# Sparse attention with scores from three products of rounded parts, the parts made by GpSimd

## What is computed

```
q = (c_q @ w_uq).reshape(B, S, DSA_HEADS, DSA_QK_DIM)     # 16 heads of 64
...
_, idx = lax.top_k(score, topk)                            # 128 keys for each query
...
q_lat = jnp.einsum('bqhd,hdc->bqhc', q_b, w_uk)
s = jnp.einsum('bqhc,bqkc->bqhk', q_lat, kv_sel).astype(jnp.float32) * (DSA_QK_DIM ** -0.5)
s = jnp.where(valid[:, :, None, :], s, -jnp.inf)
p = jax.nn.softmax(s, axis=-1).astype(kv_sel.dtype)
o_lat = jnp.einsum('bqhk,bqkc->bqhc', p, kv_sel)
o = jnp.einsum('bqhc,hcv->bqhv', o_lat, w_uv)
...
return o @ w_out
```

## Time and profile before

| | |
|---|---|
| time, median of 3 runs | 1359.1 us (1358.92 to 1359.27) |
| profiled execution | 1357.8 us, of which the span of the trace is 1356.1 us |
| PE busy | 1294.5 us, 95% of the span |
| DVE, ACT, POOL busy | 910.8, 606.4, 160.2 us |
| mean granted TensorE clock | 0.986 of full speed |
| first scores in the trace | 865.5 us |
| steady attention, one pair of heads | 9.3 to 9.5 us |
| first matmul of the output projection | 950.7 us |

### The profile page before, as it was taken

How to read it: one execution, slowest core, us unless ns; L and a number is a source line. 1 busy time by engine, 2 the same in 40 slices (tenths; PEclk the granted TensorE clock), 3 DMA queues, 4 the chain that set the end, 5 groups by cost and what they waited for, 6 DMA issues and landing times. The chain is left out here.

```text
span 1356.1 us, 18327 instructions
## 1 busy us (share of the span) xinstructions
PE 1294.5 (95%) x6915; PEld 1062.6 (78%) x6915; DVE 910.8 (67%) x1588; ACT 606.4 (45%) x1141; POOL 160.2 (12%) x172
## 2 busy tenths in 40 slices
PE   3799999999999999999999999999999999999998
PEld 3668788889887888887788876666888888888886
DVE  4878787647566888678875759877465474457245
ACT  3256774545453332233234655587353342333231
POOL 1001120104401111102000001231010001000000
PEclk9799999989999999999999999999999999999999
DMA  9644523110508896879643120001136368336321
GB/s 323 201 166 149 193 63 94 64 62 1 187 31 323 225 241 241 242 217 242 244 166 94 39 79 32 31 32 33 62 108 174 102 145 217 111 76 155 95 92 63
DMA packets 111913, 183.56 MB, mean 135 GB/s; under 512 B 9933, under 2 KB 74714, under 8 KB 111578
## 3 DMA queue, kind: packets, MB, share of 16 engines
q1 hardware_dynamic: 87930, 107.01, 24.1%
q0 software_dynamic: 23904, 75.50, 20.1%
HBM read 178.31 MB, written 4.19 MB: 135 GB/s over the span
## 5 line engine op out<-in xcount | busy, mean ns | idle before, releaser
L411 PE MATMUL ps<-h_hi,w_hi 128*128 128x512 f32 x872 | 344.5, 395 | 0.4 <-ACT tmp L1066 0.4
L413 PE MATMUL ps<-h_hi,w_lo 128*128 128x512 f32 x872 | 341.3, 391 | 0.0
L412 PE MATMUL ps<-h_lo,w_hi 128*128 128x512 f32 x872 | 341.0, 391 | 0.0
L395 DVE TENSOR_TENSOR w_lo<-raw,w_hi 128x1024 fp32r<-128x1024 f32 x140 | 170.6, 1223 | 153.9 <-ACT w_hi L389 153.0
L413 PEld LDWEIGHTS ps<-h_hi,w_lo 128*128 128x128 f32 x872 | 164.7, 189 | 35.0
L411 PEld LDWEIGHTS ps<-h_hi,w_hi 128*128 128x128 f32 x872 | 164.9, 189 | 33.8 <-issue 0.5
L412 PEld LDWEIGHTS ps<-h_lo,w_hi 128*128 128x128 f32 x872 | 165.0, 189 | 33.5
L389 ACT ACTIVATE w_hi<-raw 128x1024 fp32r<-128x1024 f32 (+1 forms) x142 | 148.2, 1051 | 29.5 <-DMA raw<-in_ffn_w_in_dram 23.5
L514 DVE SCALAR_TENSOR_TENSOR ada_acc<-ada_in,c_act,ada_acc 128x512 f32<-128x512 f32 x154 | 115.6, 750 | 4.2
L2291 ACT ACTIVATE silu_g<-ps 128x512 f32<-128x512 f32 x44 | 26.1, 593 | 120.3 <-PE ps L413 110.9
L1072 DVE SCALAR_TENSOR_TENSOR tmp<-conv_u,conv_t,tmp 128x512 f32<-128x512 f32 x72 | 54.1, 752 | 35.6 <-ACT tmp L1066 33.5
(11 more groups left out here) (429 smaller groups left out, 2601.5 us busy)
## 6 DMA issues: line engine op xcount, KB each, us to landing
raw<-in_ffn_w_in_dram SPq DMA_DIRECT2D x44, 1024.0 KB, 6.8
ada_in<-in_ada_w_dram POOLq DMA_DIRECT2D x40, 1024.0 KB, 7.0
raw<-in_gdn_w_in_dram SPq DMA_DIRECT2D x16, 1024.0 KB, 5.8
x_sum<-in_ffn_w_out_dram POOLq DMA_DIRECT2D x10, 1024.0 KB, 11.3
ada_in<-in_ffn_w_out_dram POOLq DMA_DIRECT2D x10, 1024.0 KB, 8.6
raw<-in_ffn_w_out_dram POOLq DMA_DIRECT2D x8, 1024.0 KB, 8.5
raw<-in_ffn_w_out_dram SPq DMA_DIRECT2D x12, 512.0 KB, 3.8
ada_in<-in_ada_w_dram SPq DMA_DIRECT2D x4, 1024.0 KB, 9.4
```

The costliest lines, as they stand in the source:

```text
L395: ops.tensor_tensor(lo, raw_tile(s, kc) if src is None else src, f32(hi), ALU.subtract).then_inc(lo_done, 1)
L411: nc.tensor.matmul(out_, hi[:, k, :], r_hi[:, k, :], start=k == 0, stop=False)
L412: nc.tensor.matmul(out_, hi[:, k, :], r_lo[:, k, :], start=False, stop=False)
L413: last = nc.tensor.matmul(out_, lo[:, k, :], r_hi[:, k, :], start=False, stop=k == kc - 1)
```

## The change

- The scores of a unit are now three products of rounded parts for each head: q_hi·k_hi, q_hi·k_lo, q_lo·k_hi, accumulated in the same bank; six `F32R` matmuls instead of two float32 ones. The order is product by product, and within a product head 0, then head 1.
- The parts are made by GpSimd, pair by pair, in the new `parts_pool`: two copies to `qk_hi` (q and k, two buffers by `i % 2`, in the place of `qi_t`) and two subtractions to `qk_lo`, which lies in the place of `q_t` and `k_t`. Pairs 0 and 1 wait for the last index logits, later ones until the scores of pair `i - 2` are done. PE waits at the first unit of each pair for both low parts.
- For pairs 0 to 5 GpSimd makes `o_t_hi` and `o_t_lo` in the new `o_pool`; ACT's `o_hi` and DVE's `o_lo` remain for pairs 6 and 7. ACT's copy to `o_sb` waits, from pair 2 on, until the low part of the pair two before is made.
- GpSimd's weight work stands between these steps.

```diff
@@ att_scores
-            for a in range(2):
-                lanes = slice(DH * a, DH * a + DH)
-                last = nc.tensor.matmul(ps[:, 2 * (u % 2) + a, 0:n], q_t[lanes, i, b * P:(b + 1) * P],
-                                        k_t[lanes, i, 0:n], start=True, stop=True)
+            if b == 0:
+                pe.wait_ge(sem("parts_lo"), 2 * i + 2)
+            q_hi, k_hi = qk_hi[:, 2 * (i % 2), :], qk_hi[:, 2 * (i % 2) + 1, :]
+            q_lo, k_lo = qk_lo[0][:, i, :], qk_lo[1][:, i, :]
+            for x, (q, k) in enumerate(((q_hi, k_hi), (q_hi, k_lo), (q_lo, k_hi))):
+                for a in range(2):
+                    lanes = slice(DH * a, DH * a + DH)
+                    last = nc.tensor.matmul(ps[:, 2 * (u % 2) + a, 0:n], q[lanes, b * P:(b + 1) * P], k[lanes, 0:n],
+                                            start=x == 0, stop=x == 2)
             last.then_inc(sem("s_mm"), 1)
+
+        def parts_pool(pool, i):
+
+            pool.wait_ge(sem("proj_out"), AT_Q + i + 1)
+            pool.wait_ge(sem("proj_out"), AT_K + i + 1)
+            if i < 2:
+                pool.wait_ge(sem("logit_mm"), 3 * IH)
+            else:
+                pool.wait_ge(sem("s_mm"), NB * (i - 1))
+            for x, t in enumerate((q_t, k_t)):
+                nc.gpsimd.tensor_copy(qk_hi[:, 2 * (i % 2) + x, :], t[:, i, :]).then_inc(sem("parts_hi"), 1)
+            for x, t in enumerate((q_t, k_t)):
+                pool.wait_ge(sem("parts_hi"), 2 * i + x + 1)
+                nc.gpsimd.tensor_tensor(qk_lo[x][:, i, :], t[:, i, :], f32(qk_hi[:, 2 * (i % 2) + x, :]),
+                                        ALU.subtract).then_inc(sem("parts_lo"), 1)
@@ att_act
+                    if i >= 2:
+                        act.wait_ge(sem("h_made"), 32 + i - 1)
                     nc.scalar.activation(o_sb[:, i % 2, :], ps[:, 6 + i % 2, :], ACT.Copy).then_inc(sem("o_out"), 1)
...
-                if t >= 11 and t % NB == 3:
+                if t >= 11 and t % NB == 3 and t // NB - 2 >= O_POOL:
+                    act.wait_ge(sem("h_rounded"), 32 + t // NB - 2)
                     o_hi(act, t // NB - 2)
@@ att_dve
-                if t >= 12 and t % NB == 0:
+                if t >= 12 and t % NB == 0 and t // NB - 3 >= O_POOL:
+                    dve.wait_ge(sem("h_made"), 32 + t // NB - 3)
                     o_lo(dve, t // NB - 3)
+
+        O_POOL = 6
+
+        def o_pool(pool, i):
+
+            pool.wait_ge(sem("att_scaled"), i + 1)
+            nc.gpsimd.tensor_copy(o_t_hi[:, i, :], o_sb[:, i % 2, :]).then_inc(sem("h_rounded"), 1)
+            pool.wait_ge(sem("h_rounded"), 32 + i + 1)
+            nc.gpsimd.tensor_tensor(o_t_lo[:, i, :], o_sb[:, i % 2, :], f32(o_t_hi[:, i, :]), ALU.subtract)\
+                .then_inc(sem("h_made"), 1)
@@ block.gpsimd
+            for i in range(2):
+                parts_pool(pool, i)
             for s in range(4):
+                parts_pool(pool, s + 2)
                 out_split(pool, nc.gpsimd, 2, Q_DSA_OUT, s)
+                if s:
+                    o_pool(pool, s - 1)
             for s in range(4):
+                if s < 2:
+                    parts_pool(pool, s + 6)
                 out_hi_pool(pool, Q_DSA_OUT + 1, s)
+                if s < 3:
+                    o_pool(pool, s + 3)
```

More of the change, by code:

```diff
@@ L292, in build_trunk @@
         qi_t = fixed("qi_t", [P, 4, S], at=h_base)
+        qk_hi = fixed("qk_hi", [P, 4, S], F32R, at=h_base)
+        qk_lo = [fixed(f"qk_lo{x}", [P, 8, S], F32R, at=at) for x, at in enumerate((q_at, k_at))]
         mask = fixed("mask", [P, NB, S], at=h_base + 8192)
```

## The result

The changed kernel takes 1362.3 us in the median (1357.7 to 1366.0, 20 runs), the kernel before 1359.0 (1354.9 to 1361.6, 20 runs): ratio 1.0027, with a 95% interval from 1.0018 to 1.0036. It is slower by 3.3 us; I had forecast 1355.5, faster by 3.6. The profiled execution took 1360.5 us, with a span of 1358.6.

The account below looks back on a forecast made before the run. The prediction took PE, busy for 95% of the span, as the bound. Gains of 2.5 us for scores, 0.6 for stalls and 0.5 for the tail, 3.6 us in all, gave 1355.5 us; range 1353.5 to 1361.5.

Parts of the forecast that it names:

- POOL's new work: Parts made on GpSimd: 7.9 us of a 9.0 us pair, all hidden; nothing counted for DVE's key picking beside it.
- Rival 3: Attention pairs with a weight quarter: POOL is late, about +4 us, 1359.5 us; chance 0.11.
- The scores: Attention scores: three rounded passes, array halves side by side, save 0.28 us a pair; 2.5 us with the first units.
- Rivals 1 and 2: Scores: array halves not side by side, 1371 us, chance 0.11; or weight loads wait within each half, 1361.4, chance 0.11.
- ACT and DVE relieved: Outputs' parts moved to POOL: stalls before the 384-key transposes go, 0.6 us; ACT's copy behind the last scores, 0.5 us.
- Rival 4: Attention: ACT or DVE keeps the old pace, PE waits for copies `p_t`, only 1.6 us gained, 1357.5 us; chance 0.07.
- 2.0 + 0.6 + 0.5: Attention: cheaper scores in pairs 1 to 7, transpose stalls gone in five pairs, ACT's shorter path behind the last scores.
- The 0.55: Pair 0's last two score units, at 1.2 GHz: gain in us from one pass less, cut from 0.75.
- The sum: Whole kernel: 2.5 + 0.6 + 0.5 = 3.6 us gained, a median of 1355.5 us.

Follow-up runs that it names:

- hold_parts: The changed kernel, but GpSimd begins the parts of pair 0 only when DVE has written the mask of block 2; 1355.6 us, ratio 0.9977.
- parts_alone: The kernel before, with POOL's eight instructions for the parts of pairs 0 and 1 added and their results unused; 1366.2 us, ratio 1.0063.
- hold_scores_only: hold_parts, with ACT and DVE making the parts of all outputs again, as in the kernel before; 1354.1 us, ratio 0.9960.
- hold_again: hold_parts executed a second time, unchanged; 1354.8 us, ratio 0.9967.
- before_again: The kernel before run once more, unchanged, for its trace; 1355.4 us in one run.
- tail_filled: hold_parts with ten unused transposes in PE's waits behind the last scores; 1352.6 us, ratio 0.9960, and 1353.7 us, 0.9955, when repeated.
- one_pair_early: The changed kernel with only pair 0's parts ahead of the mask of block 2, pair 1's waiting for it; 1359.9 us, ratio 1.0006.
- parts_gaps: The changed kernel, but each of POOL's eight instructions for pairs 0 and 1 waits for the end of the one before; 1355.0 us, ratio 0.9974.

## Why the prediction was wrong, point by point

**The step that failed** stands under "POOL's new work": DVE picks keys at that time and is on the critical chain, "so I count nothing". The place and the danger were right; the proof was taken from one kind of instruction. MATCH_REPLACE8 isn't slowed by POOL, which is true. DVE's chain in that stretch holds one instruction of another kind, the mask of block 2, and its start fell among POOL's eight. That is +6.8 us, measured three ways: 7.19 - 0.36 in the trace, 1362.3 - 1355.6 = 6.7 from the changed kernel to hold_parts, and +7.3 in parts_alone. Rival 3 looked for POOL being late; none of the rivals had POOL in DVE's way.

**The sign was in my own rows.** The earlier trace rows give the cast L705 as 1042 to 1511 ns, and the prediction used only the 1.04. The timeline of the kernel before, DVE and then POOL, has its cause:

```profile
914.96 1.02 DVE L2988 TENSOR_TENSOR o_t_lo<-o_sb,o_t_hi 128x512 fp32r<-128x512 f32 x1
```

```profile
914.39 2.49 POOL L705 CAST late_dsa<-raw 128x1024 fp32r<-128x1024 f32 x2
```

This subtraction takes 0.69 us in the other pairs. Here it waits until POOL's first cast ends, at 915.4, and POOL's second cast then takes 1.51 in place of 1.04 us. Each side loses time to the other there. With that row the question for the forecast would have been: which DVE instructions from SBUF to SBUF lie on the path beside POOL's new work? There is one that costs 6.8 us, and the parts of the row sums, which reach the path in one pair for 0.3.

**The scores** were right: forecast 0.48, 0.57, 0.72, 0.90, measured 0.48, 0.55, 0.71, 0.89 us, -0.32 for a pair in place of -0.28. Here the spacing of full-array matmuls could be carried over to the two half arrays. Rivals 1 and 2 fall, with the records side by side and no bare loads.

**ACT and DVE relieved.** Forecast 0.12 us for a pair, measured 0.14 alone and 0.25 on top of the new scores (9.15 to 8.90), because without it ACT is the bound. Rival 4 was real, and it is this half of the change that kept it away: in hold_scores_only a pair is 0.25 us longer.

**Pairs and tail together.** From the first turn of the row sums to the last, 61.06 us before and 58.02 after: -3.0. The prediction's terms for that stretch were 2.0 + 0.6 + 0.5 = 3.1. That they agree so closely is partly luck: most pairs gain 0.5 us, more than forecast, and the one with the long cast only 0.2. **The start**: 17.9 us in three kernels with old scores at full clock, 17.1 in hold_parts and hold_again, -0.75. The 0.55 was worked out for the lower clock, so the two aren't the same measure.

**The sum** comes out for the kernel without the collision: 1355.6 and 1354.8 us measured, 1355.5 forecast. Part of that is luck too. From the start of the mask to the projection hold_parts and hold_again take 89.0 and 89.1 us, before_again 92.9 at full clock, so 3.8 to 3.9 us are gained there, and both lose 1.6 and 1.8 us again in the transfer wait below, which none of the kernel before's traces has. What the prediction doesn't treat is that the clock there varies. The earlier trace rows show the first scores at 0.52, and I took that as given. In the changed kernel, where DVE comes 7 us late, PE waits 9.1 us for `v_tok` in place of 2.4, and the first units run at the lower level:

```profile
867.74:877.98 10.24, 3.09 (x14) 2.08 (x14) 6.86 (x22) 3.94 (x14) 0.31 (x1) 0.50 0.00 0
```

PE is busy for 3.09 of 10.24 us, and the clock is 0.50. In hold_parts the stretch from 867 to 877 is at 1.00. The column "start" shows what the lower level costs: with the new scores 17.1 us at full clock, 18.4 to 21.6 elsewhere. All six traces with a mask of 3.5 us or more have the lower level there, but so have six of the eleven others: tail_filled, which up to there is hold_parts, takes 18.4 and 20.7 us with a mask of 0.36. So it isn't shown that DVE's delay brings the clock down. The medians leave room for a small further loss: one_pair_early lost 3.2 us by its mask and is 4.3 us behind hold_parts, while the changed kernel is 6.7 behind it with a mask longer by 6.8.

**What stays open.** The wait for a weight transfer, about 2 us in the changed kernel's first trace:

```profile
1009.03 13.51 DMA raw<-in_ffn_w_in_dram
```

It is in the chain of six of the twelve kernels' traces that have the new scores and in none of the five others. The transfers are issued at the same distance from PE's work as in the kernel before, where the slowest of three took 12.2 us. From the last matmul of the output projection to the last of the kernel these six take 353.6 to 355.0 us, the other eleven traces 353.0, so the wait costs 0.6 to 2.0 us, 1.6 and 1.8 in hold_parts and hold_again. Whether the change brings it or chance does wasn't settled.

## What to carry to other kernels

Before work goes to GpSimd "because it is idle", list every VectorE instruction on the critical path that will run beside it, by kind: those with two SBUF operands, casts and tensor_scalars from SBUF to SBUF were shut out here; MAX8, MATCH_REPLACE8, and those that read one operand from PSUM were not. Put GpSimd's work behind such an instruction (hold_parts, -6.7 us), or leave gaps between its instructions (parts_gaps, the same gain for 0.12 us each). When a duration is sometimes half as long again, as in the earlier trace rows, look at what ran beside it before you average it.

The version with the lowest median is tail_filled, hold_parts with PE's last waits filled: 1352.6 and 1353.7 us, 0.9960 and 0.9955 of the kernel before.

## What the runs showed of the hardware

- A tensor_scalar of VectorE, 0.36 us alone, took 3.5 us beside four GpSimd instructions without gaps and 7.2 us beside eight, and 0.50 us when these had gaps of 0.07 us.
- Rounded (`F32R`) products on 64 rows run in both halves of the array at once: six products of 512 columns in 0.89 us, though each has a weight load of its own.
- Casts and subtractions of 128x8, 0.17 us each alone, took 0.26 to 1.24 us beside GpSimd's parts, and in hold_again this lengthened a pair from 8.90 to 9.28 us.
- The granted clock at the start of the output projection fell to the lower level (0.53 over the first 3.4 us in hold_parts) in 11 of 14 executions with waits of 0.3 to 1.0 us in PE's work ahead of it, for 1.5 to 2.8 us of time, and in none of 3 with these filled.
